# A decoder trunk on one core: the experts' rounded weight units get a ring of six instead of four

## The reference

```python
def top2_moe(h, router_w, router_b, wg, wu, wd):
    t = h.reshape(b * s, d)
    logits = (t @ router_w) + router_b
    top_v, top_i = lax.top_k(logits, TOP_K)               # 2 of 8
    gates = jax.nn.softmax(top_v, axis=-1)
    combine = sum(one_hot(top_i, N_EXPERTS) * gates[..., None], axis=1)
    for e in range(N_EXPERTS):
        out = out + combine[:, e:e + 1] * swiglu(t, wg[e], wu[e], wd[e])

def swiglu(h, wg, wu, wd):
    return (jax.nn.silu(h @ wg) * (h @ wu)) @ wd
```

## Time and profile before

| | us |
|---|---|
| median of 3 runs | 1495.96 |
| lowest and highest run | 1488.74, 1496.12 |
| the profiled execution, its own time | 1490.59 |
| span of that profile, first to last instruction | 1488.8 |
| experts' loop and item 7, as part of the span | about 492 to 1468 |

### The profile page before, as it was taken

How to read it: one execution, slowest core, us unless ns; L and a number is a source line. 1 busy time by engine, 2 the same in 40 slices (tenths; PEclk the granted TensorE clock), 3 DMA queues, 4 the chain that set the end, 5 groups by cost and what they waited for, 6 DMA issues and landing times.

```text
span 1488.8 us, 20198 instructions
## 1 busy us (share of the span) xinstructions
PE 1430.2 (96%) x7131; PEld 1169.6 (79%) x7131; DVE 1262.4 (85%) x1432; ACT 1000.1 (67%) x1188; POOL 19.8 (1%) x60
## 2 busy tenths in 40 slices
PE   7999999999999999999999999999999999999994
PEld 5875899996955788788788878878878877887883
DVE  5796887776768898898898989889889889889997
ACT  2523444354333788888888888888888888887883
POOL 1000000000000000000000000000000000001000
PEclk8999999999998999999999999999999999999998
DMA  9993678876572599999999999999999999999960
GB/s 363 395 403 143 224 289 326 298 269 253 215 297 89 217 390 356 364 386 355 368 372 365 365 362 391 359 362 375 362 367 372 361 368 371 374 358 378 410 252 30
DMA packets 203457, 482.18 MB, mean 324 GB/s; under 512 B 6928, under 2 KB 31614, under 8 KB 203402
## 3 DMA queue, kind: packets, MB, share of 16 engines
q1 hardware_dynamic: 198832, 470.31, 84.2%
q0 software_dynamic: 1584, 5.77, 1.0%
q10 hardware_dynamic: 2986, 5.38, 1.0%
HBM read 475.67 MB, written 5.77 MB: 323 GB/s over the span
## 4 chain that ended last, share of the span: by engine, by line
PE 84%; DVE 7%; ACT 6%; issue 3%; DMA 1%; ACTq 0%; DVEq 0%; SPq 0%
PE ps L1590 24%; PE ps L1592 23%; PE ps L1591 23%; ACT w_hi L809 2%; PE ps L1751 2%; PE ps L1928 2%; DVE low L1257 2%; PE ps L1607 2%; DVE ada_acc L950 1%; ACT h_t L840 1%; PE ps L1708 1%; PE ps L1552 1%; DMA raw<-in_w_ada_dram 1%; PE ps L1570 1%; ACT L809 1%
## 5 line engine op out<-in xcount | busy, mean ns | idle before, releaser
L1257 DVE TENSOR_TENSOR low<-raw,w_hi 128x1024 fp32r<-128x1024 f32 x672 | 790.3, 1220 | 67.7 <-ACT w_hi L809 53.1
L809 ACT ACTIVATE w_hi<-raw 128x1024 fp32r<-128x1024 f32 x672 | 701.3, 1062 | 132.2 <-PE ps L1592 127.8
L1590 PE MATMUL ps<-w_hi,h_lo 128*128 128x512 f32 x896 | 356.6, 398 | 10.3 <-DVE low L1257 9.8
L1592 PE MATMUL ps<-w_hi,h_hi 128*128 128x512 f32 x896 | 349.8, 390 | 0.0
L1591 PE MATMUL ps<-low,h_hi 128*128 128x512 f32 x896 | 349.1, 390 | 0.0
L1590 PE MATMUL ps<-w_hi,hid_lo 128*128 128x512 f32 x536 | 211.4, 394 | 7.4 <-DVE low L1257 4.9
L1590 PEld LDWEIGHTS ps<-w_hi,h_lo 128*128 128x128 f32 x896 | 168.2, 188 | 54.0 <-DVE low L1257 19.7
L1591 PE MATMUL ps<-low,hid_hi 128*128 128x512 f32 x536 | 208.8, 390 | 0.0
L1592 PE MATMUL ps<-w_hi,hid_hi 128*128 128x512 f32 x536 | 208.8, 390 | 0.0
L1592 PEld LDWEIGHTS ps<-w_hi,h_hi 128*128 128x128 f32 x896 | 168.2, 188 | 36.3
L1591 PEld LDWEIGHTS ps<-low,h_hi 128*128 128x128 f32 x896 | 168.5, 188 | 33.1
(11 more groups left out here) (335 smaller groups left out, 1423.2 us busy)
## 6 DMA issues: line engine op xcount, KB each, us to landing
raw<-in_moe_w_gate_dram SPq DMA_DIRECT2D x56, 2048.0 KB, 9.3
raw<-in_moe_w_up_dram SPq DMA_DIRECT2D x56, 2048.0 KB, 9.6
raw<-in_moe_w_down_dram SPq DMA_DIRECT2D x56, 2048.0 KB, 9.2
raw<-in_w_ada_dram SPq DMA_DIRECT2D x20, 2048.0 KB, 9.0
raw<-in_w_in_dram SPq DMA_DIRECT2D x6, 2048.0 KB, 16.0
raw<-in_ffn_w_gate_dram SPq DMA_DIRECT2D x11, 1024.0 KB, 8.2
raw<-in_ffn_w_up_dram SPq DMA_DIRECT2D x11, 1024.0 KB, 10.5
raw<-in_ffn_w_down_dram SPq DMA_DIRECT2D x11, 1024.0 KB, 9.5
```

The source lines that it names most:

```text
L809: act.activation(w_hi[:, (FF_UNITS + k) % SRING, :], raw[moe_slot(m)][:, (k % 4) * UNIT:(k % 4 + 1) * UNIT], ACT.Copy).then_inc(unit_hi, 1)
L1257: dve.tensor_tensor(low[moe_slot(m)][:, part], raw[moe_slot(m)][:, part], w_hi[:, q, :].bitcast(F32), ALU.subtract).then_inc(unit_lo, 1)
L1590: pe.matmul(o, x_lo, hi, start=first, stop=False, skip_group_check=True)
L1592: return pe.matmul(o, x_hi, hi, start=False, stop=last, skip_group_check=True)
```

## The change

The ring of rounded units becomes six (ERING, HEAD = 6). The four buffers of `w_hi` stay; the fifth is `hx_lo0`, which held the rest of the mixer input, the sixth is `e_hi5`, which takes the second half of the memory of `x_sb`. Because of that, what used the second half of `x_sb` in item 7 (rows fetched by POOL, the product in `y_tmp`) goes to `slot_rows`. All the steps that stand behind a unit move two units later in ACT's and DVE's order (6 to 8, 9 to 11, 80 to 82 and so on), so that they keep their place against PE; those at the end of an item now stand among the units 0 to 4 of the next one. `turned` is cut into two halves, behind units 55 and 58. The two copies of the result move from behind unit 1 to behind unit 4 of the next item. The first `code_rows` moves behind unit 7, the `add_rows` to units 34 to 69. In the head, units 4 and 5 stand between the scaling of item 0's tokens and the loop on ACT, and ahead of `residual` on DVE.

```diff
-HEAD = 4
+ERING = 6
+HEAD = 6
-TURNED_AT = 54
+TURNED_AT = (55, 58)
...
-        x_sb = sb("x_sb", [P, TT, D])
+        x_both = ExitStack()
+        x_sb = sb("x_sb", [P, TT, D], stack=x_both)
+        x_both.close()
+        sb("x_first", [P, D])
+        e_hi5 = sb("e_hi5", [P, D], F32R)
...
+        y_first, y_second = (x_sb[:, 0, :], slot_rows[:, :]), (gate1[:, :], ada_bias[:, :])
+        e_hi = [w_hi[:, k, :] for k in range(SRING)]
+        e_hi += [hx_lo0[:, :, :].rearrange("p c t -> p (c t)"), e_hi5[:, :]]
...
-                act.wait_ge(unit_used, i * E_UNITS + (FF_UNITS + k - SRING + 1))
-                act.activation(w_hi[:, (FF_UNITS + k) % SRING, :],
-                               raw[moe_slot(m)][:, (k % 4) * UNIT:(k % 4 + 1) * UNIT], ACT.Copy).then_inc(unit_hi, 1)
+                act.wait_ge(unit_used, i * E_UNITS + (FF_UNITS + k - ERING + 1))
+                act.activation(e_hi[k % ERING], raw[moe_slot(m)][:, (k % 4) * UNIT:(k % 4 + 1) * UNIT],
+                               ACT.Copy).then_inc(unit_hi, 1)
...
             gathered(0)
+            for k in range(4, HEAD):
+                moe_hi(0, k)
...
-                    after.setdefault(moe_first_unit(j) + 6, []).insert(0, ("silu", j))
+                    after.setdefault(moe_first_unit(j) + 8, []).insert(0, ("silu", j))
...
-                    after.setdefault(TURNED_AT, []).append(("turned", 0))
-                    after[E_UNITS - 5] = [("turned_hi", 0)]
-                after[E_UNITS - 4] = [("first_half", E_STEPS - 1)]
-                after[E_UNITS - 2] = [("second_half", E_STEPS - 1)]
+                    for part in range(2):
+                        after.setdefault(TURNED_AT[part], []).append(("turned", part))
+                    after[E_UNITS - 3] = [("turned_hi", 0)]
+                after[E_UNITS - 2] = [("first_half", E_STEPS - 1)]
+                after[E_UNITS] = [("second_half", E_STEPS - 1)]
+                after[E_UNITS + 4] = [("rows_out", 0)]
...
-                for k in range(HEAD if head else 0, E_UNITS):
-                    moe_hi(i, k)
+                for k in range(HEAD if head else 0, E_UNITS + HEAD):
+                    if k < E_UNITS:
+                        moe_hi(i, k)
+                    elif tail:
+                        moe_hi(i + 1, k - E_UNITS)
...
-                    for n, k in enumerate((39, 44, 50, 56, 62, 68, 74, 80)):
+                    for n, k in enumerate((34, 39, 45, 50, 54, 58, 63, 69)):
                         after.setdefault(k, []).append(("add", (n // 4, n % 4)))
```

More of the change, by code:

```diff
@@ L834, in _, with turned @@
             gathered(0)
-            def turned(i):
+            for k in range(4, HEAD):
+                moe_hi(0, k)
+            def turned(i, part):
                 act.wait_ge(xg_mm, i + 1)
-                for c in range(KC):
+                for c in range(4 * part, 4 * part + 4):
                     e = act.activation(xg[:, c, :], ps[:, 5 + c // 4, (c % 4) * P:(c % 4 + 1) * P], ACT.Identity,
                                        scale=modf[:, 3, 1, c:c + 1], bias=modf[:, 3, 0, c:c + 1])
-                e.then_inc(xg_ready, 1)
+                if part == 1:
+                    e.then_inc(xg_ready, 1)
             def turned_hi(i):
@@ L885, in item @@
                             act.activation(hid_hi[:, T:], ps[:, 2, T:], ACT.Copy).then_inc(hid_hi_ready, 1)
+                        elif what == "rows_out":
+                            act.wait_ge(unit_used, i * E_UNITS + (FF_UNITS + E_UNITS))
+                            if tail:
+                                act.wait_ge(rows_stored, i * 16 + 16 * TT)
+                            for half in range(2):
+                                if tail:
+                                    act.activation(y_out[:, half * 512:(half + 1) * 512], ps[:, 3 + half, :],
+                                                   ACT.Copy).then_inc(y_ready, 1)
+                                else:
+                                    act.activation(y_hi[half], ps[:, 3 + half, :].rearrange("p (f n) -> p f n", f=4),
+                                                   ACT.Copy).then_inc(y_ready, 1)
                         else:
@@ L1370, in item @@
                 for j in range(E_STEPS):
[L1371 removed]
+                    after.setdefault(moe_first_unit(j) + 11, []).append(("hid", j))
                     if j < E_STEPS - 1:
[L1373 to L1374 removed]
+                        after.setdefault(moe_first_unit(j + 1) + 8, []).append(("hidt", j))
+                after.setdefault(E_UNITS - 2, []).append(("first_half", E_STEPS - 1))
                 if tail:
[L1376 to L1377 removed]
+                    after[E_UNITS - 1] = [("turned_lo", 0)]
+                after.setdefault(E_UNITS, []).append(("second_half", E_STEPS - 1))
                 if head and not tail:
[L1379 removed]
+                    for n, k in enumerate((7, 9, 12)):
                         after.setdefault(k, []).append(("code", n))
[L1381 removed]
+                    for n, k in enumerate((34, 39, 45, 50, 54, 58, 63, 69)):
                         after.setdefault(k, []).append(("add", (n // 4, n % 4)))
@@ L1384, in item @@
                     gathered(i)
-                for k in range(HEAD if head else 0, E_UNITS):
-                    moe_lo(i, k)
+                for k in range(HEAD if head else 0, E_UNITS + HEAD):
+                    if k < E_UNITS:
+                        moe_lo(i, k)
+                    elif tail:
+                        moe_lo(i + 1, k - E_UNITS)
                     for what, j in after.get(k, ()):
@@ L1483, in add_rows @@
                 m.then_inc(y_added, 1)
+            for k in range(4, HEAD):
+                moe_lo(0, k)
             residual(2, 1)
```

41 lines of the change are left out of this document (11 added, 30 removed).

## The result

| | before | after |
|---|---|---|
| median of 4 runs, us | 1494.63 | 1465.58 |
| lowest and highest | 1488.74, 1496.12 | 1464.19, 1467.98 |
| ratio after / before, 95% interval | | 0.982 (0.9801 to 0.9839) |
| the profiled execution | 1490.59 | 1464.99 |

The change makes the kernel 1.8% faster. The forecast was 1473, the range 1464 to 1487.

The account below looks back on a forecast made before the run. PE was taken to bound the kernel, losing 22.9 us to late units (6 x 2.27 + 7 x 0.99 + 2.36); 1495.96 less 22.9 gave 1473 us, range 1464 to 1487.

Parts of the forecast that it names:

- The sum: Whole kernel: all 22.9 us of PE pauses in the experts go, giving 1467.7 us profiled and a 1473 us median.
- A pause costs its bracket plus 0.29 us: PE in the experts: each pause costs its shown wait plus 0.29 us, so a shown 0.74 costs 1.03 us.
- The walk through the item change: Item change, unit by unit: smallest margin 1.6 us at unit 9; three pauses go, 2.27 us, six times.
- Step 4: Eight activations hold ACT 2.73 us, PE short by 0.70; longer lead alone removes 0.99 us, seven times.
- Item 7: Last item: the single 1.03 us pause ahead and the 0.86 us one behind the first `code_rows` go.
- End of an item: `first_half`, `second_half`, `turned_lo` move two units later with the same PE waits: cost nothing, bounds 0 to 2.3 us.
- other buffers: Fifth and sixth ring buffers: the DVE instruction takes as long on them, cost zero.
- loads: ACT reaches loads two units earlier; landing 10.3 us against 25.8 available, margin 15 us, cost zero.
- The loads as the bound: Rival: 369 GB/s is the loads' ceiling, the item stays at 122.4 us and the time at 1496; chance 0.06.
- The pauses only move: Rival: DVE does not rebuild the lead before an item's end, half the gain returns, 1484.5 us; chance 0.11.
- Copies stuck behind a load: Rival: at the item change a late load holds up the result copies, store and next loads, 1545 us; chance 0.03.

Follow-up runs that it names:

- run 6: Changed kernel plus two additional ACT activations of 1024 columns, output unread, before the result copies at the item change: 1471.53 us.
- run 2: Changed kernel with ACT only four units ahead of PE, every step two units earlier, new places kept: 1478.27 us.
- run 3: Changed kernel with ACT five units ahead of PE, every step one unit earlier, result copies behind unit 3: 1466.94 us.
- run 5: Changed kernel plus one additional ACT activation of 1024 columns, output unread, before the result copies at the item change: 1469.41 us.
- Run 1: Changed kernel, six units of lead kept, but scaling activations in one piece, copies behind unit 3, item 7's sums in old places plus two: 1466.27 us.
- run 7: Changed kernel without the first of three matmuls of each half unit of the experts, so part of the product is missing: 1385.44 us.
- run 4: Changed kernel with six units of lead, but `silu`, `hidt` and `hid` back behind the units of the kernel before: 1489.45 us.

## Why the prediction was right, point by point

**The sum.** 22.9 us of pauses were to go, 24.5 went in the experts. The profiled execution was forecast at 1467.7 and took 1464.99: 1.6 us come from the experts, 1.3 from the stretch ahead of them, 0.3 go the other way. The forecast of the median, 1473, was 7.4 above the measured 1465.58, near the lower end of the range. The weak step there is the last: the offset of 5.4 us between the profiled execution and the median of the three runs shown was carried over to the changed kernel, as if it were a property of the kernel. It was chance. All 24 executions of the kernel before that were timed have a median of 1492.3, 1.7 above the profiled one, and the changed kernel's median lies 0.6 above its profiled execution. Against that median the changed kernel's is 26.7 us lower, not 29 as in the table; the account rests on the experts' 24.5.

**A pause costs its bracket plus 0.29 us** held in each place: the item's period fell by 3.35 us, forecast 2.27 + 0.99 = 3.26. It holds for the bracket only; for a unit that is late by the walk the surcharge is 0.18 us (run 6).

**The walk through the item change** gave for units 5, 6 and 9 the times 3.6, 5.85 and 10.65 us; the trace has 3.57, 5.94 and 10.69. Runs 2, 3, 5 and 6 tested it with other leads and with additional work, and all came out within about 0.2 us per item.

**Step 4** was right in its result, but the prediction named only the longer lead as the cause. Run 1 shows that the lead is enough with the block in one piece, run 2 that two halves are enough with four units of lead.

**Item 7** is the term that was sized too small: 1.03 + 0.86 = 1.9 us, measured 2.9. The prediction took only the two long pauses there, because it left the waits of the weight loads out, as "the same wait again, overlapping with it". They are not all the same. In the earlier trace rows PEld waits for `low` 32 times and PE 28 times, and PEld once more for `hid_lo`. Up to the end of item 6 both have 26 such waits; in item 7 of the kernel before (1347 to 1468) PE has two, and the weight loads have these:

```profile
PEld ps L1590 <- DVE low L1257: 3.4, 6, 1.2
PEld ps L1590 <- DVE hid_lo L1405: 0.2, 1, 0.2
```

The five that PE's row does not have are at units 7, 45, 57, 81 and 82. There DVE is so little late that the wait ends about when the matmul before is modelled to end, and PE's row carries no bracket. One of them, of the kernel before:

```profile
1428.39 0.39 PE L1590 MATMUL ps<-w_hi,h_lo 128*128 128x512 f32 x1
1429.21 0.19 PEld L1590 LDWEIGHTS ps<-w_hi,h_lo 128*128 128x128 f32 x1 [0.41 <-DVE low L1257]
1429.21 0.50 PE L1590 MATMUL ps<-w_hi,h_lo 128*128 128x512 f32 x1
1430.02 0.40 PE L1590 MATMUL ps<-w_hi,h_lo 128*128 128x512 f32 x1
```

The two distances are 0.82 and 0.81 instead of 0.68, together 0.27 us. Counted so, unit 7 costs 0.12, unit 45 0.24, unit 57 0.27 and units 81 and 82 together 0.24 us: 0.87 of the missing 1.0. In the changed kernel all of them are gone. That DVE is short there is also in the earlier trace rows, 38 of 40 us busy; the places where it is short late in the item lie among its additional sums.

**End of an item, other buffers, loads:** costed at nothing, and nothing they cost. The same DVE instruction takes 1219, 1220 and 1221 ns with `w_hi`, `hx_lo` and `e_hi`. A load lands in 7.7 to 10.2 us (median of an item, items 0 to 6), in the kernel before in 7.9 to 10.3: nothing changed there, and the 10.3 and 8.4 us of the two stretches shown are within that.

**The rivals.** *The loads as the bound* is out: 379 GB/s over an item, and 413 in run 7. The Trainium skill's figure of about 358 GB/s for a core (DMA: Bandwidth & Descriptors, Specifications) is below both, so here the measurement decides; only one core of the chip was at work, and no run here had a second one load beside it. *The pauses only move* did not happen, but run 4 shows that it would have, and by this rival's own mechanism (DVE without lead at the item's end, PE waiting for `hid_lo`), had the steps not been shifted along with the ring. *Copies stuck behind a load* did not happen; the longest landing in the experts of the changed kernel is 17.8 us.

## What to carry to other kernels

A ring between two engines covers blocks of other work on the producer, but not as long as its depth times the consumer's unit: four units of 1.36 us are 5.44 us, and a block of 2.73 us in step 4 was 0.70 too long for them, since a buffer can be filled only when PE is done with it, and each unit then has to pass through the producers (here 0.95 us on ACT, 1.2 us on DVE and the signals between). So walk the worst place once with the durations of the trace, unit by unit; here the walk was right to about 0.2 us, and said that five units are enough with the new places. A deeper ring was worth almost nothing here while the steps that wait for the consumer stayed where they were in the producers' order (run 4): move them by as many units as the ring has grown. Count the consumer's pauses and multiply, with those of its weight loads that have no counterpart among its matmuls, and do not look at its busy share, which moved by one point in a hundred here. And a resource that is slower than the bound by a little can hide behind its buffers for a whole run: look at whether its times grow from item to item, as in run 7.

## What the runs showed of the hardware

A wait of PE costs more than the trace's bracket: after each pause the first two matmuls start 0.34 us apart instead of 0.23, and together with the 0.16 us by which the modelled end of a matmul lies behind the next one's undisturbed start, that makes 0.29 us on top, with rounding. With a third less work for PE, in run 7, the loads of this core ran at a steady 413 GB/s over 200 us while their landings grew by about 1.4 us an item, so more than that they did not give there. And the experts repeated to 0.3 us in 951 between four kernels without pauses, while the start of item 0 moved by 3.2 us.
